# A decay-scaled triangle and a normalization in a Mamba-2 scan, written by ScalarE in place of VectorE

## The chip, the core and the metric

The kernel runs on one core of one Trainium2 chip. The metric is the device time of one execution in microseconds (us). PE is TensorE, DVE is VectorE, ACT is ScalarE, POOL is GpSimd and SP is SyncE. A profile is of one execution, taken by the hardware profiler.

## The reference, cut to what matters

The program is a two-layer decoder trunk over 512 tokens and 1024 features in float32: sparse attention, SwiGLU, a Mamba-2 (SSD) mixer, SwiGLU. The change is in the mixer's chunked scan, of which this is the core (chunks of 128 tokens, 4 groups of 8 heads, head size 64, state size 128):

```
def step(state, inp):
    cum = jnp.cumsum(dtc * A, axis=1)
    seg = cum[:, :, None] - cum[:, None]
    L = jnp.exp(jnp.where(tril, seg, -jnp.inf))
    cb = jnp.einsum('btgn,bsgn->btsg', cc, bc)
    y_diag = jnp.einsum('btsgh,bsghp->btghp', cb[..., None] * L, xdt)
    y_off = jnp.einsum('btgn,bghpn->btghp', cc, state) * jnp.exp(cum)[..., None]
    ...
    return new_state, y_diag + y_off
...
y = y + d_skip[..., None] * xs
yg = y * silu(z)                                   # per group of 512 features
yg = yg * rsqrt(mean(yg * yg) + EPS)               # over the group
return (yg * norm_w) @ w_out
```

## The kernel before, in words

Each engine has its own program, written out by hand in order; they meet only in semaphores. An engine runs its instructions in program order, so a wait holds everything behind it.

The scan runs over 16 tiles: 4 groups `g` of heads, and in each 4 chunks of tokens `k` (called tiles 0 to 3 of a group below). The group function of each engine is called for group 0, in a loop for groups 1 and 2, and for group 3 with `last=True` (`scan_groups`, L294). In every tile the engines do this:

- The decays of tile `k+1`. `build_g` (L1532) writes `Gm`: for each of 8 heads the 128x128 triangle `tri[:, 0]` times one number per partition (`dt * A` of that head), four heads (128x512) to an instruction and two instructions (`q`) to a tile. It is called two tiles ahead. PE multiplies `Gm` with a second triangle (L744) into two PSUM banks, ACT takes the exponential into `Lx` (`decays`, L1083), POOL multiplies it with the masked product of C and B (L1725).
- The inputs of tile `k+1`: POOL makes `xdt`, `dxs` and `xdd` (L1717 to L1720), ACT packs B and C (`stage`, L1076), PE multiplies and transposes them (L748, L749), DVE copies them out (`stage`, L1540).
- The output of tile `k`: PE multiplies with the state (L793), forms the state's increment (L796), and does eight small products with `Lx` (L802). DVE scales, adds and gates: L1591, L1593 and L1594 (the state), L1600, L1602, and L1605, which multiplies by `zs` and signals `y_done`.
- The normalization of tile `k`: ACT sums the squares (L1124), DVE makes the mean (L1550), POOL the power -1/2 (`rstd`, L1636, signal `y_rs`), and DVE multiplies the 128x512 tile `ybuf` by it (`scale_y`, L1552, an instruction at L1555, signal `y_scaled`). PE transposes the result (L756), DVE copies it to `yT` (L1561).

PE has other work in the scan: the projection `z` of the next group (L772), 24 products of 128x512 to a tile, in thirds of 8, placed around the scan's own products. They fill one PSUM bank; ACT copies it out (`z_copy`, L1096) before the next tile's may start (signal `evac`). In tile 0 of a group all three thirds stand at the end. The `z` products of tile 0 need new weights from their 13th on, those of tile 3 release a weight buffer. A weight chunk is split by ACT (`split_hi`, L827) and then DVE (`split_lo`, L1152), in tile 0 and in tile 3. In tile 0 of groups 1 to 3 ACT also turns `zraw` into `zs` by Silu over 2048 columns (L1116), with a load of the activation table before it. Group 3 has no `z`; there ACT and DVE split parts of `yT` instead (L1121, L1611), and after tile 3 the output projection starts (L354 to L356 with `yh`, `yl`).

ACT's order in a tile is `z_copy` of the tile before, the weight split (tile 0), the exponentials, `stage`, Silu (tile 0) or the weight split (tile 3) or L1121 (last group), then the sum of squares. DVE's is mean, `stage`, `scale_y` of the tile before, `build_g`, the weight split (tiles 0 and 3), L1591 to L1605, L1561, L1611 (last group).

Of the kernel before, what the change touches and what calls it, by code (L numbers as in the profile page):

```python
# [27 lines left out]
ALU = mybir.AluOpType  # L28
ACT = mybir.ActivationFunctionType
AX = mybir.AxisListType.X  # L30

P = 128
SEQ, DM = 512, 1024
TT = SEQ // P
# [7 lines left out]
SH, SG, SHP, SP_, SN = 32, 4, 8, 64, 128  # L42
# [67 lines left out]
def trunk(nc, wstream, xT_in, cols_in, rows_in, pos_in, cw1_in, cw2_in, ident_in, tri_in, cmask_in, out):  # L110
    with ExitStack() as ctx:
# [177 lines left out]
        def after(engine, semaphore, value):  # L289

            if not isinstance(value, int) or value > 0:
                engine.wait_ge(semaphore, value)

        def scan_groups(engine, group, enter=None, leave=None):  # L294

            group(0, False)
            with engine.Fori(0, SG - 2) as i:
                if enter:
                    enter(i)
                group(i + 1, False)  # L300
            if leave:
                leave()
            group(SG - 1, True)
# [515 lines left out]
        def _(act):  # L819
            A = act.activation  # L820

            def split_hi(n, i=None, per=0):

                act.wait_ge(landed[n % 2], 16 * (n // 2 + 1) if i is None else i * (8 * per) + 16 * (n // 2 + 1))
                if n >= 2:
                    act.wait_ge(products, at(2 * (n - 1), i, 2 * per))
                A(wh[:, n % 2, :], wraw[:, n % 2, :], ACT.Copy).then_inc(hi_done, 1)  # L827
# [248 lines left out]
            def stage(g, j):  # L1076

                c = j % TT
                after(act, y_mm, g * 8 + 2 * (j - 3))
                A(bc[:, c, :, :], BCf[:, :, bass.ds(g + j // TT, 1), c * P:(c + 1) * P].rearrange("p b a n -> p (b a) n"),  # L1080
                  ACT.Copy).then_inc(staged, 1)

            def decays(g, j):  # L1083
                for q in range(2):
                    act.wait_ge(seg_mm, g * 8 + (2 * j + q + 1))
                    after(act, y_mm, g * 8 + 2 * (j - 1))
                    A(Lx[:, j % 2, q, :, :], ps[:, q, :].rearrange("p (h t) -> p h t", h=4), ACT.Exp
                      ).then_inc(seg_exp, 1)

            def z_copy(g, tt):  # L1090

                if tt in (-1, 3):
                    act.wait_ge(products, g * 4 + (2 * n0 + 4 + tt + 1))
                else:
                    act.wait_ge(z_mm, g * 3 + (tt + 1))
                A(zraw[:, tt % TT, :], ps[:, 5, :], ACT.Copy, scale=stat[:, 4 + tt % TT:5 + tt % TT]).then_inc(evac, 1)  # L1096

            def group(g, last):
                first = isinstance(g, int) and g == 0
                for k in range(TT):  # L1100
                    if k:
                        if not last:
                            z_copy(g, k - 1)
                    elif not first:
                        z_copy(g, -1)
                    if k == 0:
                        split_hi(n0 + 3, g, 2)
                    if k < 3 or not last:
                        decays(g, k + 1)
                    if k < 2 or not last:  # L1110
                        stage(g, k + 2)
                    if k == 0:
                        if not first:
                            act.wait_ge(evac, g * 4 + (t0 + 4))
                            act.wait_ge(y_done, g * 4)
                            A(zs[:, :, :], zraw[:, :, :], ACT.Silu).then_inc(z_silu, 1)  # L1116
                    if k == 3 and not last:
                        split_hi(n0 + 4, g, 2)
                    if last:
                        act.wait_ge(yT_done, 9 + k)  # L1120
                        A(yh[:, k, 0:12, :], yT[:, k, 0:12, :], ACT.Copy).then_inc(yh_done, 1)  # L1121
                    act.wait_ge(y_done, g * 4 + (k + 1))
                    after(act, y_sq, g * 4 + k)
                    A(ysq[:, :], ybuf[:, k % 2, :], ACT.Square, accum_out=yst[:, k % 2, 0:1]).then_inc(y_sq, 1)  # L1124
            stage(0, 0)
            stage(0, 1)
            decays(0, 0)
            split_hi(n0 + 2)
            for tt in range(TT):
                act.wait_ge(products, 2 * n0 + 3 + tt // 2)  # L1130
                A(zs[:, tt, :], ps[:, 2 + tt, :], ACT.Silu, scale=stat[:, 4 + tt:5 + tt]).then_inc(evac, 1)
            scan_groups(act, group)
            act.wait_ge(yT_done, 4 * SG)
            A(yh[:, :, 12:16, :], yT[:, :, 12:16, :], ACT.Copy).then_inc(yh_done, 1)
            residual("ssm_out")
# [4 lines left out]
        def _(dve):  # L1140
# [388 lines left out]
            n0 = CHUNK["z"]  # L1529


            def build_g(g, j):  # L1532

                for q in range(2):
                    after(dve, seg_mm, g * 8 + (2 * j + q - 1))
                    at_ = g * SHP + ((j // TT) * SHP + (j % TT) * SH + 4 * q)
                    TTo(Gm[:, q, :, :], tri[:, 0, :].unsqueeze(1).broadcast_to([P, 4, P]),
                        dtb[:, 1, bass.ds(at_, 4)].unsqueeze(2).broadcast_to([P, 4, P]), ALU.mult).then_inc(g_built, 1)

            def stage(g, j):  # L1540

                dve.wait_ge(cb_mm, g * 4 + (j + 1))
# [5 lines left out]
            def y_mean_square(g, j):  # L1548
                dve.wait_ge(y_sq, g * 4 + (j + 1))
                TS(yst[:, j % 2, 1:2], yst[:, j % 2, 0:1], 1.0 / GW, EPS, ALU.mult, ALU.add).then_inc(y_var, 1)  # L1550

            def scale_y(g, j):  # L1552
                dve.wait_ge(y_rs, g * 4 + (j + 1))
                y = ybuf[:, j % 2, :]
                TS(y, y, yst[:, j % 2, 2:3], None, ALU.mult).then_inc(y_scaled, 1)  # L1555

            def to_features(g, j):
                dve.wait_ge(yT_mm, g * 4 + (j + 1))
# [8 lines left out]
            def group(g, last):  # L1567
                first = isinstance(g, int) and g == 0

                def per_head(n, c):  # L1570
                    return ex[:, n, bass.ds(g * SHP + c * SH, SHP)].unsqueeze(2).broadcast_to([P, SHP, SP_])
                for k in range(TT):
                    if k or not first:
                        y_mean_square(g, k - 1)
                    if k < 3 or not last:
                        stage(g, k + 1)
                    if k or not first:
                        scale_y(g, k - 1)
                    if k < 2 or not last:
                        build_g(g, k + 2)  # L1580
                    if k == 0:
                        split_lo(n0 + 3, g, 2)
                    if k == 3 and not last:
                        split_lo(n0 + 4, g, 2)
                    y = ybuf[:, k % 2, :]
                    after(dve, yT_mm, g * 4 + (k - 1))
                    if k < 3:
                        dve.wait_ge(state_mm, g * 3 + (k + 1))
                    if k:
                        dve.wait_ge(y_mm, g * 8 + (2 * k + 1))  # L1590
                        V.inc(TTo(heads(y), heads(ps[:, 3, :]), per_head(0, k), ALU.mult))  # L1591
                    if k in (1, 2):
                        step(TTo(heads(state[:, :]), heads(state[:, :]), per_head(2, k), ALU.mult))  # L1593
                        TTo(state[:, :], state[:, :], ps[:, 4, :], ALU.add).then_inc(state_done, 1)  # L1594
                    if k == 0:
                        dve.tensor_copy(state[:, :], ps[:, 4, :]).then_inc(state_done, 1)
                    dve.wait_ge(y_mm, g * 8 + 2 * (k + 1))
                    dve.wait_ge(xdt_done, g * 12 + 3 * (k + 1))
                    V.wait(dve)
                    step(TTo(y, y if k else dxs[:, k % 2, :], ps[:, 2, :], ALU.add))  # L1600
                    if k:
                        step(TTo(y, y, dxs[:, k % 2, :], ALU.add))  # L1602
                    if k == 0 and not first:
                        dve.wait_ge(z_silu, g)
                    TTo(y, y, zs[:, k, :], ALU.mult).then_inc(y_done, 1)  # L1605
                    if k or not first:
                        to_features(g, k - 1)
                    if last:
                        dve.wait_ge(yh_done, k + 1)
                        dve.wait_ge(yT_done, 9 + k)  # L1610
                        TTo(yl[:, k, 0:12, :], yT[:, k, 0:12, :], yh[:, k, 0:12, :].bitcast(F32), ALU.subtract  # L1611
                            ).then_inc(yl_done, 1)
            build_g(0, 0)
            dve.wait_ge(cum_exp, 1)
            stage(0, 0)
            build_g(0, 1)
            split_lo(n0 + 2)
            scan_groups(dve, group, lambda i: V.enter(i, DVE_SCAN_STEPS), lambda: V.leave(SG - 2, DVE_SCAN_STEPS))
            y_mean_square(SG - 1, 3)
            scale_y(SG - 1, 3)  # L1620
            to_features(SG - 1, 3)
            dve.wait_ge(yh_done, TT + 1)
            TTo(yl[:, :, 12:16, :], yT[:, :, 12:16, :], yh[:, :, 12:16, :].bitcast(F32), ALU.subtract).then_inc(yl_done, 1)
# [210 lines left out]
```

## Time and profile before

| | |
|---|---|
| median of 3 runs | 1614.51 us (1613.33 to 1615.09) |
| the profiled execution | 1612.59 us, span 1610.8 us |
| PE busy | 1508.9 us (94%) |
| DVE busy | 853.7 us (53%) |
| ACT busy | 630.9 us (39%) |
| POOL busy | 261.2 us (16%) |
| mean granted PE clock | 0.982 |

The span runs from the first to the last instruction; busy shares are of the span. Times of single rows are microseconds from the span's start. The scan stands between about 943 and 1148 us.

### The profile page before, as it was taken

To read this page: it belongs to the slowest core of one execution; us is meant where nothing else is said; L and a number is where in the kernel's file an instruction comes from. 1 tells how busy PE (TensorE), PEld (TensorE's weight loads), DVE (VectorE), ACT (ScalarE), POOL (GpSimd) and SP (SyncE) were. 2 spreads that over 40 slices of the span, in tenths; PEclk is the share of its full clock that TensorE was granted. 3 is DMA by queue.
4 is the path that set the end of the run, shared out by engine and by line. 5 is a ranking of instruction groups with operands and counts; after the bars stand their busy time and mean duration, and the time that the engine had idled before them with its cause. 6 is when DMAs were issued, how large, how long until landed. Compare 5 with 4: busy or idle time off the path is not lost.

```text
span 1610.8 us, 20549 instructions
## 1 busy us (share of the span) xinstructions
PE 1508.9 (94%) x7469; PEld 1217.9 (76%) x7469; DVE 853.7 (53%) x1137; ACT 630.9 (39%) x895; POOL 261.2 (16%) x289
## 2 busy tenths in 40 slices
PE   6989889778999999999999999998799999999999
PEld 5777667656788888788788867665687888887887
DVE  4556767663444444333397758789623444444222
ACT  4445655653343433323233352444223344343111
POOL 4133242301100000001000026666211000000000
PEclk9989999999999999999999999999799999999999
DMA  7200101102222222222222220111022222222222
GB/s 310 79 27 1 53 12 40 52 1 79 79 105 98 84 104 104 80 103 104 105 105 79 102 81 27 53 52 53 4 101 79 105 79 104 91 91 104 105 105 78
DMA packets 19198, 129.47 MB, mean 80 GB/s; under 512 B 2256, under 2 KB 2896, under 8 KB 4560
## 3 DMA queue, kind: packets, MB, share of 16 engines
q1 hardware_dynamic: 19008, 126.75, 21.9%
q10 hardware_dynamic: 144, 2.10, 0.4%
q8 instruction: 30, 0.49, 0.1%
q14 instruction: 16, 0.13, 0.0%
HBM read 126.74 MB, written 2.10 MB: 80 GB/s over the span
## 4 chain that ended last, share of the span: by engine, by line
PE 82%; issue 6%; DVE 5%; POOL 5%; ACT 2%; DVEq 0%; POOLq 0%; ACTq 0%
PE ps L354 22%; PE ps L356 22%; PE ps L355 22%; PE ps L624 3%; PE ps L607 2%; PE ps L772 2%; PE ps L587 2%; POOL Lx L1725 2%; POOL sqacc L1650 1%; PE ps L550 1%; PE ps L744 1%; PE ps L603 1%; PE ps L802 1%; DVE sm L1370 1%; PE ps L551 1%
## 5 line engine op out<-in xcount | busy, mean ns | idle before, releaser
L1152 DVE TENSOR_TENSOR wl<-wraw,wh 128x2048 fp32r<-128x2048 f32 x112 | 264.5, 2362 | 274.0 <-ACT wh L827 273.9
L354 PE MATMUL ps<-xh,wh 128*128 128x512 f32 (+2 forms) x912 | 359.3, 394 | 6.1 <-DVE xl L1162 3.4
L355 PE MATMUL ps<-xl,wh 128*128 128x512 f32 (+2 forms) x912 | 356.2, 391 | 0.0
L356 PE MATMUL ps<-xh,wl 128*128 128x512 f32 (+2 forms) x912 | 356.2, 391 | 0.0
L827 ACT ACTIVATE wh<-wraw 128x2048 fp32r<-128x2048 f32 x112 | 213.9, 1910 | 185.3 <-PE ps L356 175.5
L354 PEld LDWEIGHTS ps<-xh,wh 128*128 128x128 f32 (+2 forms) x912 | 170.8, 187 | 44.3 <-issue 4.5
L356 PEld LDWEIGHTS ps<-xh,wl 128*128 128x128 f32 (+2 forms) x912 | 170.7, 187 | 37.4
L355 PEld LDWEIGHTS ps<-xl,wh 128*128 128x128 f32 (+2 forms) x912 | 170.8, 187 | 37.0 <-issue 0.7
L354 PE MATMUL ps<-hh,wh 128*128 128x512 f32 x352 | 137.9, 392 | 4.1 <-DVE hid L1232 4.1
L355 PE MATMUL ps<-hl,wh 128*128 128x512 f32 x352 | 137.6, 391 | 0.0
L356 PE MATMUL ps<-hh,wl 128*128 128x512 f32 x352 | 137.5, 391 | 0.0
L1650 POOL TENSOR_TENSOR sqacc<-sqacc,sq 128x512 f32<-128x512 f32 x32 | 44.2, 1381 | 481.9 <-ACT sq L836 480.9
L889 ACT ACTIVATE hh<-hid 128x512 f32 x44 | 27.8, 632 | 189.7 <-DVE hid L1232 189.7
L1370 DVE TENSOR_REDUCE sm<-ps 128x2 f32<-128x256 f32 (+3 forms) x64 | 52.6, 822 | 67.6 <-PE ps L545 40.9
L354 PEld LDWEIGHTS ps<-hh,wh 128*128 128x128 f32 x352 | 66.4, 189 | 18.8 <-DVE hid L1232 5.0
L982 ACT ACTIVATE PT<-ps 128x256 f32<-128x256 f32 (+3 forms) x64 | 45.0, 704 | 83.0 <-PE ps L587 82.7
L355 PEld LDWEIGHTS ps<-hl,wh 128*128 128x128 f32 x352 | 66.5, 189 | 13.9
L356 PEld LDWEIGHTS ps<-hh,wl 128*128 128x128 f32 x352 | 66.5, 189 | 13.8
L974 ACT ACTIVATE Pm<-ps,sm 128x128 f32<-128x128 f32 (+3 forms) x128 | 66.1, 526 | 9.3 <-DVE sm L1370 9.2
L885 ACT ACTIVATE gate<-gate 128x512 f32<-128x512 f32 x44 | 27.7, 632 | 102.0 <-DVE gate L1225 102.0
L1195 DVE TENSOR_TENSOR xT<-ps,xT 128x512 f32<-128x512 f32 (+1 forms) x32 | 22.1, 690 | 85.7 <-PE ps L356 77.2
L587 PE MATMUL ps<-ident,Pm 128*128 128x128 f32 x320 | 47.3, 279 | 17.7 <-DVE Pm L1381 15.9
(262 smaller groups left out, 2491.1 us busy)
## 6 DMA issues: line engine op xcount, KB each, us to landing
wraw<-wstream SPq DMA_DIRECT2D x112, 1024.0 KB, 4.8
cw<-cw_in SPq DMA_DIRECT2D x1, 4096.0 KB, 18.9
xT<-xT_in SPq DMA_DIRECT2D x4, 512.0 KB, 8.1
xT<-xT_in ACTq DMA_DIRECT2D x1, 2048.0 KB, 8.5
out<-xT SPq DMA_DIRECT2D x8, 256.0 KB, 6.5
rows<-rows_in SPq DMA_DIRECT2D x1, 276.0 KB, 10.5
tri<-tri_in SPq DMA_DIRECT2D x1, 192.0 KB, 10.5
cmask<-cmask_in SPq DMA_DIRECT2D x1, 128.0 KB, 10.0
```

What stands on the lines that cost most here:

```text
L354: mm(o, wa[0], xa[0], start=start, stop=False)
L355: mm(o, wa[0], xa[1], start=False, stop=False)
L356: return mm(o, wa[1], xa[0], start=False, stop=stop)
L587: ins = pe.transpose(ps[:, 4 + b, j * P:(j + 1) * P], Pm[:, s % 2, b, j * P:(j + 1) * P], ident[:, :])
L607: ins = mm(o, vst[:, j, b, :], PT[:, h % 2, b, j, q], start=False, stop=b == 1 and j == i)
L624: ins = mm(ps[:, 7, :], (xh, xl, xh)[pss][:, kt, t], (wh, wh, wl)[pss][:, slot, w], start=m == 0, stop=m == 23)
L827: A(wh[:, n % 2, :], wraw[:, n % 2, :], ACT.Copy).then_inc(hi_done, 1)
L974: A(Pm[:, s % 2, b, 0:w], src, ACT.Exp, bias=sm[:, 4, m + b:m + 1 + b], accum_out=sm[:, 4, m + 4 + b:m + 5 + b]).then_inc(expd, 1)
L982: A(PT[:, h % 2, :, 0:i + 1, i * P:(i + 1) * P], ps[:, 4:6, 0:(i + 1) * P].rearrange("p b (j q) -> p b j q", q=P), ACT.Copy).then_inc(pT_d ...
L1152: TTo(wl[:, s, :], wraw[:, s, :], wh[:, s, :].bitcast(F32), ALU.subtract).then_inc(lo_done, 1)
L1370: dve.tensor_reduce(sm[:, 4, m:m + 2], src.rearrange("p (b n) -> p b n", b=2) if i < 2 else src, AX, ALU.max, negate=True).then_inc(negmax, 1)
L1650: TTo(sqacc[:, :], sqacc[:, :], sq[:, mt % 2, :], ALU.add).then_inc(acc_done, 1)
```

## The change

`build_g` and `scale_y` move from DVE's program to ACT's. `build_g` becomes eight ACT instructions of 128x128 to a tile in place of two DVE instructions of 128x512: an activation Copy takes one scale for each partition, so each head is an instruction of its own. `scale_y` stays one instruction of 128x512. Their places in ACT's order are new: `scale_y` of the tile before stands first in a tile, ahead of `z_copy`; `build_g` stands between the exponentials and `stage`. At the start `build_g(0, 0)` stands behind the exponential of the cumulative sums (L1074) and ahead of `stage(0, 0)`, where DVE did it before them.

```
@@ block.scalar
+            def build_g(g, j):
+                for q in range(2):
+                    after(act, seg_mm, g * 8 + (2 * j + q - 1))
+                    at_ = g * SHP + ((j // TT) * SHP + (j % TT) * SH + 4 * q)
+                    for h in range(4):
+                        a = dtb[:, 1, at_ + h:at_ + h + 1] if isinstance(at_, int) else dtb[:, 1, bass.ds(at_ + h, 1)]
+                        ins = A(Gm[:, q, h, :], tri[:, 0, :], ACT.Copy, scale=a)
+                    ins.then_inc(g_built, 1)
+            def scale_y(g, j):
+                act.wait_ge(y_rs, g * 4 + (j + 1))
+                y = ybuf[:, j % 2, :]
+                A(y, y, ACT.Copy, scale=yst[:, j % 2, 2:3]).then_inc(y_scaled, 1)
...
                 for k in range(TT):
+                    if k or not first:
+                        scale_y(g, k - 1)
                     if k:
                         if not last:
                             z_copy(g, k - 1)
...
                     if k < 3 or not last:
                         decays(g, k + 1)
+                    if k < 2 or not last:
+                        build_g(g, k + 2)
                     if k < 2 or not last:
                         stage(g, k + 2)
...
+            act.wait_ge(dt_done, 1)
+            build_g(0, 0)
             stage(0, 0)
             stage(0, 1)
             decays(0, 0)
+            build_g(0, 1)
             split_hi(n0 + 2)
...
             scan_groups(act, group)
+            scale_y(SG - 1, 3)
@@ block.vector
-            def build_g(g, j):
-                for q in range(2):
-                    after(dve, seg_mm, g * 8 + (2 * j + q - 1))
-                    at_ = g * SHP + ((j // TT) * SHP + (j % TT) * SH + 4 * q)
-                    TTo(Gm[:, q, :, :], tri[:, 0, :].unsqueeze(1).broadcast_to([P, 4, P]),
-                        dtb[:, 1, bass.ds(at_, 4)].unsqueeze(2).broadcast_to([P, 4, P]), ALU.mult).then_inc(g_built, 1)
-            def scale_y(g, j):
-                dve.wait_ge(y_rs, g * 4 + (j + 1))
-                y = ybuf[:, j % 2, :]
-                TS(y, y, yst[:, j % 2, 2:3], None, ALU.mult).then_inc(y_scaled, 1)
...
-                    if k or not first:
-                        scale_y(g, k - 1)
-                    if k < 2 or not last:
-                        build_g(g, k + 2)
...
-            build_g(0, 0)
             dve.wait_ge(cum_exp, 1)
             stage(0, 0)
-            build_g(0, 1)
             split_lo(n0 + 2)
...
             y_mean_square(SG - 1, 3)
-            scale_y(SG - 1, 3)
             to_features(SG - 1, 3)
```

## Rows read from the trace of the kernel before

**Rows 1.** Windows: start:end, us, then each engine's busy us (instructions), PE clock, DMA
```profile
1063.60:1112.00 48.40, 44.56 (x212) 32.28 (x211) 40.80 (x51) 19.89 (x31) 30.78 (x25) 1.00 0.12 44
1112.00:1148.30 36.30, 21.11 (x82) 13.69 (x80) 33.34 (x41) 13.44 (x19) 19.11 (x15) 0.76 0.09 29
```
**Rows 2.** Instruction groups by line and form, DVE: busy us, mean ns, idle before
```profile
L1537 DVE TENSOR_TENSOR Gm<-tri,dtb 128x512 f32<-128x512 f32 x32 | 45.5, 1461 | 0.0
L1555 DVE TENSOR_SCALAR ybuf<-ybuf,yst 128x512 f32<-128x512 f32 x16 | 14.7, 917 | 2.4 <-POOL yst L1636 2.1
```
**Rows 3.** Instruction groups by line and form, ACT: the nearest form for `scale_y`
```profile
L841 ACT ACTIVATE xh<-xT,cols 128x512 fp32r<-128x512 f32 x24 | 15.8, 708 | 0.0
```
**Rows 4.** Timeline of ACT (start us, us): two 128x128 with an operand per partition
```profile
91.82 0.62 ACT L955 ACTIVATE hidK<-ps,cols 128x128 f32<-128x128 f32 x2
```
**Rows 5.** Timeline of PE, tiles 0 to 3 of group 2
```profile
1067.23 0.50 PE L772 MATMUL ps<-wh,xh 128*128 128x512 f32 x1 [2.71 <-DVE wl L1152]
...
1072.07 0.47 PE L772 MATMUL ps<-wh,xh 128*128 128x512 f32 x1
...
1087.24 1.90 PE L802 MATMUL ps<-xdt,Lx 128*128 128x64 f32 x16
...
1095.12 0.47 PE L772 MATMUL ps<-wh,xh 128*128 128x512 f32 x1
```
**Rows 6.** Timeline of DVE: end of group 1, tiles 0 and 2 of group 2
```profile
1057.43 0.69 DVE L1605 TENSOR_TENSOR ybuf<-ybuf,zs 128x512 f32<-128x512 f32 x1
...
1068.41 0.69 DVE L1605 TENSOR_TENSOR ybuf<-ybuf,zs 128x512 f32<-128x512 f32 x1
...
1088.45 0.69 DVE L1591 TENSOR_TENSOR ybuf<-ps,ex 128x512 f32<-128x512 f32 x1 [0.18 <-PE ps L802]
...
1092.03 0.69 DVE L1605 TENSOR_TENSOR ybuf<-ybuf,zs 128x512 f32<-128x512 f32 x1
```
**Rows 7.** The chain that ended last: POOL's power, and `z` of tile 1, group 1
```profile
1024.86 1.84 PE ps L772 x8
...
1059.15 0.56 POOL yst L1636
```
**Rows 8.** Timeline of ACT around the start of group 2
```profile
1058.16 0.63 ACT L1124 ACTIVATE ysq<-ybuf 128x512 f32<-128x512 f32 x1 [5.51 <-DVE ybuf L1605]
...
1058.79 0.67 ACT L1096 ACTIVATE zraw<-ps,stat 128x512 f32<-128x512 f32 x1
1059.36 1.90 ACT L827 ACTIVATE wh<-wraw 128x2048 fp32r<-128x2048 f32 x1
...
1063.85 1.91 ACT L1116 ACTIVATE zs<-zraw 128x2048 f32<-128x2048 f32 x1
```
**Rows 9.** Timeline of PE where the scan starts
```profile
948.44 1.98 PE L744 MATMUL ps<-Gm,tri 128*128 128x512 f32 x4 [0.58 <-ACT ex L1074]
...
950.51 0.47 PE L354 MATMUL ps<-wh,xh 128*128 128x512 f32 x1
```
**Rows 10.** Timeline of DVE: ends of groups 0 and 2, tiles 0 and 2 of group 3
```profile
1008.40 0.69 DVE L1605 TENSOR_TENSOR ybuf<-ybuf,zs 128x512 f32<-128x512 f32 x1
...
1105.09 0.69 DVE L1605 TENSOR_TENSOR ybuf<-ybuf,zs 128x512 f32<-128x512 f32 x1
...
1116.06 0.69 DVE L1605 TENSOR_TENSOR ybuf<-ybuf,zs 128x512 f32<-128x512 f32 x1
...
1132.74 0.69 DVE L1591 TENSOR_TENSOR ybuf<-ps,ex 128x512 f32<-128x512 f32 x1
...
1136.74 1.63 DVE L1605 TENSOR_TENSOR ybuf<-ybuf,zs 128x512 f32<-128x512 f32 x1
```
**Rows 11.** Timeline of PE: tile 2 of group 3 and the output projection's first product
```profile
1128.40 2.07 PE L793 MATMUL ps<-state,bc 128*128 128x512 f32 x2 [2.99 <-DVE ybuf L1605]
...
1148.31 0.80 PE L354 MATMUL ps<-yh,wh 128*128 128x512 f32 x1 [3.65 <-DVE yl L1611]
```
**Rows 12.** Windows (columns as in Rows 1): the products behind PE's wait in group 1
```profile
1018.20:1022.80 4.60, 4.60 (x13) 3.66 (x14) 2.58 (x5) 0.72 (x2) 2.79 (x4) 0.63 0.65 228
```

## The prediction

> **What bounds the kernel now.** I read the table of windows first. In group 2 of the scan PE is busy 44.56 of 48.40 us and DVE 40.80, ACT only 19.89; in group 3, which has no `z` products, DVE is busy 33.34 of 36.30 and PE 21.11 [rows 1]. So the scan has two stages with different limits: groups 0 to 2 go by PE, group 3 by DVE's list together with the waits between it and PE. Then the groups of instructions: what the change takes off DVE is 45.5 us of `build_g` and 14.7 of `scale_y` [rows 2], 60 us in all. That isn't the gain. The timelines say which wait ends last. In tile 2 of group 2 DVE's L1591 was itself released by PE [rows 6], so with two instructions fewer ahead of it, it starts no sooner. The one wait of PE inside groups 1 and 2 is 2.71 us for the weight split in tile 0 [rows 5].
>
> ACT is idle more than half the time, but the question is what now stands in its queue ahead of what PE needs: `z_copy` (PE's next `z` products wait for it), the weight split, and in tile 0 the Silu that L1605 waits for.
>
> **Prices of the moved work.** `scale_y`: 0.71 us, as L841, the same form [rows 3], and the next instruction starts 0.1 sooner than it ends, so 0.61 in a queue. A `build_g` instruction is 128x128 with a scale per partition. From L841's 0.708 less 384 columns at (1.91 - 0.63) / 1536 = 0.83 ns [rows 8] one alone is 0.39. Two short ones of that kind in a row took 0.62 together [rows 4], so the second adds 0.23 to 0.31. I take 0.29 from start to start, 2.3 us for the eight of a tile; ends 0.25 and 0.39 (2.0 and 3.1 us). In the loop each has its scale's address from a register, which no row shows for such short ones; that is why the upper end goes without any overlap.
>
> **1. The start.** `Gm` was ready long before; now ACT makes it after L1074. PE's L744 began at 948.44 and the products behind it at 950.51 [rows 9]. Now 2.3 us of `build_g` lie ahead, of which PE's first half of L744 (1.0 us) hides one, and `stage` behind it puts 0.2 more ahead of L748. The second half of L744 can start at about 950.8, the products at 952.0: **+1.5** (ends 1.2 and 2.3). Everything behind moves with it, since PE is full there.
>
> **2. Tiles 1 to 2 and 2 to 3 of groups 0 to 2.** A new wait stands first in ACT's tile: `scale_y` waits for `y_rs`, and `z_copy` is behind it. From `y_done` (1057.43 + 0.69 = 1058.12 [rows 6]) `z_copy` started 0.67 later [rows 8]; the power ended 1.59 later (1059.15 + 0.56 [rows 7]). Now `scale_y` starts at 1.63, `z_copy` at 2.24, ends at 2.91, and PE's next `z` products start at 2.97 after `y_done`. In tile 2 of group 2 L802 started at 1087.24, `y_done` came at 1092.72 [rows 5, 6], 5.48 later; 5.48 + 2.97 = 8.45, where PE by its own list starts `z` after 7.88 (1095.12 [rows 5]). PE so waits 0.57. As DVE's chain may run a little faster with less beside POOL, the ends are 0 and 0.6; I take 0.4, six times: **+2.4**. Behind `z_copy` stand the exponentials, `build_g`, `stage`; `Gm` and `Lx` are wanted a tile later, so they are covered.
>
> **3. Tile 3.** ACT's weight split waits for the 12th `z` product, so there was idle time of ACT before it; `build_g` (2.3) makes it about 0.4 late. DVE's half then runs after POOL's products rather than beside them, which gives 0.4 to 0.6 back: **0** (ends -0.2 and +0.6, thrice).
>
> **4. Tile 0 of groups 1 and 2.** Here ACT's queue is longest: `scale_y`, `z_copy`, split, exponentials, `build_g`, `stage`, table load, Silu. Silu ended 1063.85 + 1.91 - 1058.12 = 7.64 after `y_done` [rows 6, 8]. New: 0.96 waiting for `y_rs` (1.63 - 0.67), 0.61 for `scale_y`, 2.32 for `build_g`: 11.53. L1605 of tile 0, which started at 1068.41, 10.29 after [rows 6], now starts at 11.58 and ends at 12.27; the tail of step 2 (2.97) puts PE's `z` of tile 1 at 15.24. Before it was 1072.07 - 1058.12 = 13.95 in group 2 [rows 5, 6], so +1.3; in group 1 it was 1024.86 - 1009.09 = 15.77 [rows 7, 10], because PE's clock was granted at 0.63 behind its 2.71 us wait [rows 12]; that slow stretch would now be hidden: -0.5. Together **+0.8**. The old 2.71 us wait for the weights shrinks (DVE's split no longer stands behind `build_g`), but what it gives is taken by the wait for `z_copy` and buys nothing. PE is then idle twice, some 2 us each.
>
> **5. Group 3.** From `y_done` of group 2 (1105.78) to the output projection (1148.31) it was 42.53 us [rows 10, 11]. Tile 0 ends later for the Silu, at 12.27 against 10.97 (1116.75). From there DVE has less in its list (`scale_y` and `build_g` no longer stand ahead of L1591) and the loop is PE to DVE to PE: from L793 to L1591 4.34 us (1128.40 to 1132.74), then DVE's chain, 4.27 us where POOL was quiet (1088.45 to 1092.72 [rows 6]) and 5.63 where it read beside it (1132.74 to 1138.37 [rows 10]). I take 4.8 twice: `y_done` at 21.4 and 30.6, and from there as before 9.94 (1138.37 to 1148.31): 40.5. **-2.0** (ends -3.1 with 4.27 twice, -0.4 with 5.63). ACT's L1121 now stands behind `build_g` and ahead of the sum of squares and can hold that up, but only `stage` on DVE and POOL's inputs hang on it, and I count these as done before L1591 is released.
>
> L1605 took 1.63 us beside POOL's products in tile 2 of this group and 0.69 elsewhere [rows 10, 6]. The Trainium skill ("SBUF — State Buffer", section "SBUF: two separate sides") says that VectorE, in an instruction with two SBUF inputs, and GpSimd reading SBUF hold a shared port in turn, and that "the other fully blocks". By that rule L1602 and L1605 meet POOL's `Lx` in both tiles whatever else DVE has dropped, and the sum would be 1.6 higher than mine, 1619.6.
>
> **6. The clock.** Two more waits of about 2 us in each of groups 1 and 2 can bring the lower level as the 2.71 us one did once in two. At 0.63 twelve products took 4.6 us [rows 12] where they need 2.8 at the full level, some 1.6 to 1.8. Behind the weights it is hidden, behind `z_copy` it isn't. I add half of one: **+0.8**.
>
> **7. The end.** The last `scale_y` and its transpose lie behind the first products of the projection: 0.
>
> The sum is 1.5 + 2.4 + 0 + 0.8 - 2.0 + 0.8 = +3.5. The profiled execution took 1612.59 us (span 1610.8), which makes 1616.1; the median stands 1.9 above it, so **1618.0**.
>
> **Rivals.** *DVE was the bound (faster).* If the Silu, or whatever ACT does in tile 0, ended by 10 us after `y_done`, group 3 would lose what leaves DVE's list: four `scale_y` of 0.92 and four `build_g` instructions of 1.46 [rows 2], 9.5 us, less 1.5 of the start: 8.0, 1606.5. For it: DVE's 92% in group 3. Against it: the queue of step 4, whose length comes from rows. *The queue hides better than I think (no change).* Step 2 gives 0, group 3 gives 3.1: 1.5 + 0.8 - 3.1 = -0.8, 1613.7. For it: step 2 is a difference of 0.57 between two sums of 8. *The eight instructions don't overlap (slower still).* 0.39 each adds 0.8 to a tile: at the start, in tile 0 of groups 1 to 3, in tile 3 of groups 0 to 2 (0.6 of it) and in tile 1 of group 3: 0.8 + 2.4 + 1.8 + 0.8 = 5.8, 1623.8. For it: register addresses; against it: rows 4.
>
> **How the numbers follow.** A measurement of this kernel tells about 0.2%, 3.2 us, from no change. My forecast has a chance of 0.58, own range 1614.5 to 1622; the faster rival 0.13; no change 0.15; the slower one 0.14. Faster by over 0.2% (under 1611.3) is the first rival and a little of the second, 0.15; within 0.2% (to 1617.7) is the rest of the second and the lower part of my own range, 0.34; slower is 0.51. Range 1610 to 1625.
>
> **What would show it.** Right: eight ACT instructions at 0.29 spacing; PE waits for L1096 before its first `z` product in tiles 1 to 3, about 2 us in tile 1 and under 0.6 in the others; L1605 of tile 0 waits for the Silu, near 12.3 after `y_done`; group 3 two us shorter. Wrong: no such waits of PE, L1605 of tile 0 released by something on DVE or PE, or group 3 shorter by over 5 us.

## The result, and the profile after

The changed kernel takes 1620.93 us (median of 7 runs, 1617.74 to 1622.19), the kernel before 1615.09 beside it (7 runs, 1613.33 to 1615.64). The ratio is 1.0036 with a 95% interval of 1.0026 to 1.0045: slower by 5.8 us, and by 4.2 to 7.3 with the interval. Forecast were 1618.0 and +3.5.

The profiled execution of the changed kernel, at 1622.19 us, is the slowest of its seven, that of before (1612.59) the fastest of its own. So the two traces differ by 9.6 us, more than the medians do. Of all executions behind the medians in this text two were disturbed and are left out of the ratios, though not of the medians: one of the kernel with Silu first (2560.44 us) and one of the kernel before (1750.42). Busy time moved as meant: DVE from 853.7 to 791.6 us, ACT from 630.9 to 677.1. The two moved groups, by line and form (busy us, mean ns, idle before):

```profile
L1097 ACT ACTIVATE Gm<-tri,dtb 128x128 f32<-128x128 f32 x128 | 39.1, 397 | 0.0
L1103 ACT ACTIVATE ybuf<-ybuf,yst 128x512 f32<-128x512 f32 x16 | 11.6, 722 | 18.5 <-POOL yst L1639 18.5
```

Against [rows 2] ACT needs 51 us of busy time for what cost DVE 60, and it waits another 18.5 us for the power of POOL, sixteen times, ahead of whatever stands behind `scale_y`. (L1605 of before is L1611 in this kernel, L1725 is L1728.)

To see where the time is, I cut the scan at the same events in every trace: the first product with `dtb` on PE (L736), the first `z` product behind it, `y_done` of tile 3 of groups 0, 1 and 2 (start plus duration of the instruction that multiplies by `zs`), the first product of the output projection, and the end. All in us:

| kernel | start | to the end of group 0 | group 1 | group 2 | group 3 | rest |
|---|---|---|---|---|---|---|
| before | 3.48 | 58.58 | 49.03 | 47.66 | 42.53 | 462.49 |
| changed | 4.95 | 58.93 | 52.22 | 51.09 | 42.13 | 463.80 |
| only `build_g` moved | 4.96 | 58.05 | 45.33 | 45.33 | 40.88 | 464.00 |
| only `scale_y` moved | 3.48 | 58.63 | 47.34 | 47.40 | 41.02 | 462.41 |
| changed, `z_copy` first | 4.95 | 58.06 | 46.38 | 46.39 | 40.57 | 463.46 |
| changed, Silu first | 4.95 | 58.89 | 48.47 | 48.48 | 41.53 | 463.91 |
| changed, 10 idle products | 4.95 | 58.95 | 50.34 | 50.34 | 42.38 | 463.19 |
| changed, 7 idle products | 4.95 | 58.91 | 49.41 | 49.43 | 41.51 | 462.81 |
| changed, last `build_g` early | 4.94 | 58.91 | 49.41 | 50.98 | 41.14 | 463.62 |
| only `build_g` moved, start on DVE | 3.48 | 58.06 | 45.33 | 45.34 | 41.46 | 463.05 |
| changed, `z_copy` first, start on DVE | 3.48 | 58.09 | 46.40 | 46.39 | 41.56 | 463.65 |
| moved in group 3 alone | 3.48 | 58.61 | 49.03 | 47.69 | 38.06 | 463.18 |
| best | 3.48 | 58.05 | 45.32 | 45.32 | 39.58 | 463.98 |

Not in the table is what lies ahead of the scan. The same code there ended between 944.10 us (last `build_g` early) and 951.65 (only `build_g` moved) in these thirteen traces, and the rest, also the same code, took 462.41 to 464.00. So a stage of one trace may be set against the same stage of another, but the total of one execution says little. Group 3 with the same instructions took 42.13, 42.38 and 41.51 us (changed, 10 and 7 idle products), so less than a microsecond there is no difference either.

The waits of PE in the scan of the changed kernel (who waited for whom, us in total, times, longest):

```profile
PE ps L744 <- ACT Gm L1097: 8.1, 3, 3.4
PE ps L793 <- DVE ybuf L1611: 6.2, 2, 4.6
PE ps L772 <- ACT zraw L1111: 6.2, 2, 3.1
PE ps L354 <- DVE yl L1617: 3.6, 1, 3.6
PE ps L772 <- DVE wl L1175: 1.6, 2, 0.8
```

The 2.71 us wait for the weights [rows 5] is down to 0.8, and 3.1 us for `z_copy` stands in its place, in tile 1 of groups 1 and 2. ACT's timeline at the start of group 2 shows why (start us, us):

```profile
1063.42 0.63 ACT L1143 ACTIVATE ysq<-ybuf 128x512 f32<-128x512 f32 x1 [5.13 <-DVE ybuf L1611]
...
1064.99 0.72 ACT L1103 ACTIVATE ybuf<-ybuf,yst 128x512 f32<-128x512 f32 x1 [0.85 <-POOL yst L1639]
1065.61 0.67 ACT L1111 ACTIVATE zraw<-ps,stat 128x512 f32<-128x512 f32 x1
1066.18 1.90 ACT L827 ACTIVATE wh<-wraw 128x2048 fp32r<-128x2048 f32 x1
1067.99 1.07 ACT L1087 ACTIVATE Lx<-ps 128x512 f32<-128x512 f32 x2
1068.94 2.45 ACT L1097 ACTIVATE Gm<-tri,dtb 128x128 f32<-128x128 f32 x8
...
1073.01 1.91 ACT L1135 ACTIVATE zs<-zraw 128x2048 f32<-128x2048 f32 x1
1075.75 0.63 ACT L1143 ACTIVATE ysq<-ybuf 128x512 f32<-128x512 f32 x1 [0.83 <-DVE ybuf L1611]
...
1077.32 0.72 ACT L1103 ACTIVATE ybuf<-ybuf,yst 128x512 f32<-128x512 f32 x1 [0.85 <-POOL yst L1639]
1077.94 0.67 ACT L1111 ACTIVATE zraw<-ps,stat 128x512 f32<-128x512 f32 x1
```

From `y_done` (1063.38) to here ACT has no idle time but 0.85 us for the power, twice, and 0.83 for L1611 (the lines left out are short ones and a load of the activation table, 1.28 us). Compare [rows 8]: there `z_copy` came 0.67 after `y_done`, here 2.23, and the Silu ends 11.54 after it, not 7.64. On DVE and PE the same stretch reads:

```profile
1075.02 0.69 DVE L1611 TENSOR_TENSOR ybuf<-ybuf,zs 128x512 f32<-128x512 f32 x1 [3.42 <-ACT zs L1135]
```

```profile
1070.46 0.50 PE L772 MATMUL ps<-wh,xh 128*128 128x512 f32 x1 [0.79 <-DVE wl L1175]
...
1078.66 0.50 PE L772 MATMUL ps<-wh,xh 128*128 128x512 f32 x1 [3.11 <-ACT zraw L1111]
```

`y_done` of tile 0 now hangs on the Silu, and `z` of tile 1 starts 15.28 after `y_done` of the group before (13.95 before).

What comes behind those two waits is PE at the lower of its two clock levels (0.50 where it holds for a whole window, 1.2 of 2.4 GHz). Windows of the changed kernel (columns as in [rows 1]), behind the wait in group 1 and in group 2:

```profile
1026.44:1029.00 2.56, 2.56 (x6) 2.08 (x7) 0.00 (x0) 2.55 (x5) 2.25 (x3) 0.50 0.00 0
1029.00:1032.91 3.91, 3.91 (x7) 1.94 (x7) 0.00 (x0) 2.42 (x9) 1.88 (x2) 0.57 0.00 0
...
1078.60:1081.00 2.40, 2.33 (x9) 1.88 (x9) 0.00 (x0) 2.37 (x5) 2.10 (x3) 0.83 0.00 0
1081.00:1084.00 3.00, 3.00 (x6) 1.20 (x4) 0.00 (x0) 2.64 (x10) 2.09 (x2) 0.57 0.00 0
```

### The profile page after: what moved, and what is told of

The parts are those of the page before. It is cut to its first block, busy times and chain, and to the rows that moved or that the text cites. A ratio compares the mean times of both kernels' runs of the same rounds, so it can differ in the third digit from the quotient of the medians.

```text
span 1620.4 us, 20685 instructions
## 1 busy us (share of the span) xinstructions
PE 1513.7 (93%) x7469; PEld 1218.5 (75%) x7469; DVE 791.6 (49%) x1089; ACT 677.1 (42%) x1039; POOL 243.3 (15%) x289
## 4 chain that ended last, share of the span: by engine, by line
PE 82%; issue 7%; POOL 4%; DVE 4%; ACT 3%; DVEq 0%; POOLq 0%; ACTq 0%
PE ps L354 22%; PE ps L356 22%; PE ps L355 22%; PE ps L624 3%; PE ps L607 2%; PE ps L772 2%; PE ps L587 2%; POOL Lx L1728 1%; PE ps L744 1%; PE ps L802 1%; PE ps L550 1%; POOL sqacc L1653 1%; PE ps L603 1%; PE ps L551 1%; DVE sm L1393 1%
## 5 line engine op out<-in xcount | busy, mean ns | idle before, releaser
L1175 DVE TENSOR_TENSOR wl<-wraw,wh 128x2048 fp32r<-128x2048 f32 x112 | 258.4, 2307 | 304.6 <-ACT wh L827 304.4
## 6 DMA issues: line engine op xcount, KB each, us to landing
cmask<-cmask_in SPq DMA_DIRECT2D x1, 128.0 KB, 10.4
```

The source lines that it names most:

```text
L1175: TTo(wl[:, s, :], wraw[:, s, :], wh[:, s, :].bitcast(F32), ALU.subtract).then_inc(lo_done, 1)
```

## The experiments

My theory after the result: nothing that was moved is dear. ACT's order makes one queue of the wait for `y_rs`, `scale_y`, `z_copy`, `build_g` and the Silu, and PE waits at its end, at times with a lowered clock behind it. The rivals stand in the expectations.

**One part alone.** The first kernel has `scale_y` back on DVE, the second `build_g`:

```diff
# only build_g moved: ACT
-                    if k or not first:
-                        scale_y(g, k - 1)
... the last scale_y (tile 3 of group 3) goes from here too
# and DVE, behind stage(g, k + 1), as before
+                    if k or not first:
+                        scale_y(g, k - 1)
... and the last one
```

> The changed kernel with scale_y back on DVE: only build_g is on ACT. Theory (what costs is one queue on ACT in tile 0: the wait for y_rs, scale_y and build_g all stand ahead of the Silu, and z_copy stands behind scale_y): build_g alone puts the Silu's end at 7.6 + 2.3 = 10.0 us after y_done, just what L1605 had before, so nothing is left of the 3 us waits of PE for z_copy and only the start (+1.5) and a gain in group 3 remain: 1613.5 to 1616.5, no difference from before. Rival (the eight short instructions cost by themselves, wherever they stand; parts add up): the larger part of the 5.8 us remains, 1618 to 1620.

```diff
# only scale_y moved: ACT
-                    if k < 2 or not last:
-                        build_g(g, k + 2)
# and DVE, as before (build_g(0, 0) and build_g(0, 1) too)
+                    if k < 2 or not last:
+                        build_g(g, k + 2)
```

> The changed kernel with build_g back on DVE (the start too): only scale_y is on ACT. Theory: the six waits of PE for z_copy in tiles 2 and 3 (0.2 to 0.6 us each) stay, +1 to +2.4, no long wait in tile 1, since the Silu ends near 9.2 after y_done; group 3 gets back three scale_y of DVE, -3: 1613 to 1616. Rival (parts add up): what build_g alone leaves of the 5.8 us, 1617 to 1619.

Measured: 1607.29 us (ratio to before 0.995, interval 0.9937 to 0.9963) and 1608.02 (0.9959, 0.9945 to 0.9972). Both expectations of mine are missed, on the good side, and the rival falls altogether: each part alone gains 7 us, and both together lose 6. Most of why they gain is in the waits of PE in groups 1 and 2: before, one of 2.71 us for the weights in each [rows 5]. In group 1 with `build_g` alone, and with `scale_y` alone, all that is left is:

```profile
PE ps L772 <- ACT zraw L1106: 0.9, 1, 0.9
```

```profile
PE ps L772 <- DVE wl L1160: 1.2, 1, 1.2
PE ps L772 <- ACT zraw L1101: 0.8, 1, 0.8
```

Without `build_g` (2.98 us) or `scale_y` (1.26) ahead of the weight split DVE has the weights sooner; I had expected tile 1 to start when it did before, though that start was itself late by the 2.71 us. With `build_g` alone both groups take 45.33 us: 2.3 less than before in group 2 and 3.7 in group 1, where before had the clock's fall as well. Group 3, which has none of these waits, gives another 1.6 and 1.5 us in the table.

**ACT's order.** One kernel has the changed kernel's `z_copy` ahead of `scale_y`, so that it doesn't wait for POOL's power; another has `build_g` behind the Silu.

```diff
+                    if k:
+                        if not last:
+                            z_copy(g, k - 1)
+                    elif not first:
+                        z_copy(g, -1)
                     if k or not first:
                         scale_y(g, k - 1)
-                    if k:
-                        if not last:
-                            z_copy(g, k - 1)
-                    elif not first:
-                        z_copy(g, -1)
```

> The changed kernel with z_copy ahead of scale_y in ACT's order, nothing else. Theory: PE's waits for z_copy go in tiles 1 to 3 (3.1 us in tile 1 twice, 0.2 to 0.5 six times), and with them the fall of the clock behind the two long ones (1.3 to 1.7 each, in some executions): 1620.9 - 6 - 1 - 2 = 1612 to 1615. Rival (the Silu behind build_g sets the pace by holding y_done, not z_copy): PE then waits for y_done at L793 instead; gain under 2 us, 1619 to 1621.

```diff
-                    if k < 2 or not last:
-                        build_g(g, k + 2)
                     if k < 2 or not last:
                         stage(g, k + 2)
                     if k == 0:
                         ... Silu
+                    if k < 2 or not last:
+                        build_g(g, k + 2)
```

> The changed kernel with build_g behind the Silu in tile 0 (and in the other tiles behind stage), z_copy still behind scale_y. Theory: y_done of tile 0 comes 2.3 us sooner, PE's two long waits shrink from 3.1 to 0.8 and the clock holds: 1620.9 - 4.6 - 1.5 = 1614 to 1616.5. Rival (z_copy behind scale_y is the whole cost, or Gm is then late for PE's L744): 1619 to 1621.

`z_copy` first: 1608.61 (0.9967, 0.9953 to 0.998). Swapping two instructions of ACT gives 12.3 us back, more than I expected, and makes a kernel slower than before into a faster one. By the table 3.0 us a group of it is waiting (46.4 us against the 49.4 that a group of the changed kernel takes at the full clock, see below), and some 4.5 is the clock. Its waits in group 1 are these, and its clock doesn't fall behind them:

```profile
PE ps L772 <- ACT zraw L1111: 1.3, 1, 1.3
PE ps L772 <- DVE wl L1175: 0.4, 1, 0.4
```

Silu first: 1616.96 (1.0013, 1.0003 to 1.0024), 4.0 less than the changed kernel and a little above the range that I expected. Group 1 takes 48.47 us, and what is left stands in the waits of PE over the whole scan: the Silu is out of the way, but now `Gm` comes late.

```profile
PE ps L744 <- ACT Gm L1097: 9.8, 5, 6.9
...
PE ps L772 <- ACT zraw L1111: 2.6, 2, 1.3
```

So of the two, the order of `z_copy` is the larger part: the wait for POOL's power belongs behind whatever PE waits for.

**The clock.** Into PE's wait for `z_copy` I put products whose result nobody reads. The wait isn't shortened by them.

```diff
# tile 1 of groups 1 and 2; ten, in the second kernel seven
+                    if k == 1 and not last and not (isinstance(g, int) and g == 0):
+                        for _ in range(10):
+                            mm(ps[:, 3, 0:256], ident[:, :], tri[:, 0:2, :].rearrange("p a b -> p (a b)"), start=True, stop=True)
                     z_at(0)
```

> The changed kernel with ten more products of 128x256 on PE, thrown away, in tile 1 of groups 1 and 2, where PE waits 3.1 us for z_copy. They take some 2.1 us and put no result anywhere that is read. Theory: PE's clock isn't lowered behind that wait any more, and the lowered stretch (0.50 to 0.60, 1.3 to 2.3 us of PE's time in each group) goes: groups 1 and 2 from 52.2 and 51.1 us to about 49.5, 1620.9 - 3 to 4 = 1617 to 1618. Rival (the clock isn't part of it; the length of the wait alone is): the same 1620.9, or more by what the products delay.

> As with ten thrown-away products in tile 1 of groups 1 and 2 of the changed kernel, but seven. Ten took 4.1 us of PE where 3.1 were idle, and groups 1 and 2 came to 50.3 us each; seven take 2.9. Theory: the clock is held all the same, groups 1 and 2 come to 49.4 us, 1617.0 to 1618.2. Rival (fewer let the clock fall in some executions): as the changed kernel, 1619 to 1621.

Ten: 1619.15 (1.0037, 1.0023 to 1.0052), groups 1 and 2 at 50.34 us. The trace has the full clock, but the ratio is that of the changed kernel, so by its time this kernel misses what I expected. The products ran longer than I had reckoned, 4.14 us to the next start where I took 2.1, and longer than the wait of 3.1:

```profile
1022.44 4.48 PE L790 MATMUL ps<-tri,ident 128*128 128x256 f32 x20
1026.58 0.58 PE L772 MATMUL ps<-wh,xh 128*128 128x512 f32 x1
```

Seven: 1616.18 (1.0010, 0.9999 to 1.0020), a little below what I expected, groups 1 and 2 at 49.41 and 49.43. The same 49.41 stands in group 1 of the kernel with the last `build_g` early, which has no such product: there the clock held by itself in that execution (windows; before, at and behind the wait):

```profile
1018.00:1023.00 5.00, 2.11 (x8) 0.92 (x6) 1.94 (x5) 3.32 (x5) 1.70 (x3) 1.00 0.25 103
1023.00:1026.00 3.00, 2.77 (x10) 1.99 (x11) 0.00 (x0) 2.97 (x6) 2.69 (x3) 1.00 0.00 0
```

So 49.4 us is a group's length with the full clock, and its fall cost 2.8 and 1.7 us in the two groups of the changed kernel's trace. With seven idle products the kernel is 4.7 us faster by the medians (1620.93 against 1616.18; the kernel before had 1615.09 and 1614.41 beside them). That the whole difference is the clock's isn't shown; single runs of the kernel with seven products went up to 1622.88. Nor is it shown beyond doubt that the products hold the clock: it was full behind all four waits with them, and behind one of four without them (two in the changed kernel's trace, two in that of the last `build_g` early).

**Group 3.** The `build_g` for its tile 3 goes first in tile 1, where ACT waits for the power anyway, and from its old place:

```diff
                 for k in range(TT):
+                    if last and k == 1:
+                        build_g(g, 3)
                     if k or not first:
                         scale_y(g, k - 1)
```

> The changed kernel with one build_g moved: in the last group, the one for tile 3 stands first in tile 1, ahead of scale_y and the exponentials. Theory (group 3 gained nothing because PE's L744 for tile 3, which waits 2.9 us for Gm, stands ahead of L793 of tile 2): that wait goes and group 3 falls from 42.1 to about 40 us, 1618 to 1619.5. Rival (group 3 is held by DVE beside POOL, whatever Gm does): no change, 1620.5 to 1621.5.

1619.34 (1.0029, 1.0018 to 1.0040), whose interval overlaps that of the changed kernel; in the traces group 3 falls from 42.13 to 41.14 us, half of what I expected and little more than the same code differs by. PE in the changed kernel, and then in this one:

```profile
1126.84 1.12 PE L793 MATMUL ps<-state,bc 128*128 128x512 f32 x2 [1.61 <-DVE ybuf L1611]
...
1134.21 3.26 PE L744 MATMUL ps<-Gm,tri 128*128 128x512 f32 x4 [2.90 <-ACT Gm L1097]
...
1137.90 1.17 PE L793 MATMUL ps<-state,bc 128*128 128x512 f32 x2
```

```profile
1120.71 2.07 PE L793 MATMUL ps<-state,bc 128*128 128x512 f32 x2 [1.07 <-DVE ybuf L1613]
...
1126.85 1.96 PE L744 MATMUL ps<-Gm,tri 128*128 128x512 f32 x4 [0.34 <-ACT Lx L1087]
1130.97 1.12 PE L793 MATMUL ps<-state,bc 128*128 128x512 f32 x2 [1.84 <-DVE ybuf L1613]
```

L793 of tile 2 no longer stands behind the wait for `Gm`, but now waits for `y_done` itself. Part of the missing half is the clock: from 1120.7 to 1124.0 it was granted at 0.50. L793 of tile 1 took 2.07 us in this execution and 1.12 in the other, and DVE's L1599, which PE releases, started 4.60 us behind it (1125.31) in place of 2.96.

**The start, and where the gain can be had.** Three more kernels. The first two are the `build_g` kernel and the `z_copy` one with the first two `build_g` back on DVE (the diff is that of the change, reversed, at the start):

> build_g on ACT, scale_y on DVE (1607.3 as such), and the first two build_g before the groups back on DVE. Theory: the start's 1.5 us is plainly on the path, since ACT makes Gm while PE waits: 1605.3 to 1606.3. Rival (something behind it hides the start, such as the wait for the Silu of z at the end of that stage): 1607 to 1607.5.

> Both moved, z_copy ahead of scale_y (1608.6 as such), and the first two build_g back on DVE. Theory: -1.5, 1606.6 to 1607.6. Rival as for the other: 1608.3 to 1608.9.

1605.87 (0.9948, 0.9935 to 0.9961) and 1608.66 (0.9961, 0.9948 to 0.9973). The start is 3.48 us again in both traces. The first median is 1.4 us lower, as expected, the second no lower; with intervals of some 4 us neither tells 1.5 us from nothing, so the gain is shown by the start's column of the table alone. In the second kernel's trace group 3 took 41.56 us against 40.57, with the same instructions in it. What differs is where the clock was low. PE with `z_copy` first, and then with the start on DVE too:

```profile
1114.68 2.07 PE L793 MATMUL ps<-state,bc 128*128 128x512 f32 x2 [2.01 <-DVE ybuf L1611]
...
1122.05 2.29 PE L744 MATMUL ps<-Gm,tri 128*128 128x512 f32 x4 [1.77 <-ACT Gm L1097]
```

```profile
1113.80 1.13 PE L793 MATMUL ps<-state,bc 128*128 128x512 f32 x2 [1.69 <-DVE ybuf L1616]
...
1121.16 3.40 PE L744 MATMUL ps<-Gm,tri 128*128 128x512 f32 x4 [2.90 <-ACT Gm L1097]
```

`Gm` is there at the same time after `y_done` of group 2 in both. In the first the lower level falls into tile 1 and L744 of tile 2 runs at the full one; in the second it falls on L744 (granted clock 0.60 from 1121 to 1124), and L793 behind it starts 23.00 us after that `y_done`, not 22.06.

> The kernel before, with the move made in the last group alone: scale_y on ACT there, and the build_g of its tile 3 on ACT, first in tile 1; everything else on DVE as before. Theory (of the gain of the single moves, groups 1 and 2 make most by PE's shorter wait for the weights, and group 3 some 1.5 to 2.5 us): 1612 to 1613.5. Rival (the gain lies in group 3, where DVE was 92% busy): 1608 to 1610.

```diff
# ACT, the kernel before
+                    if last and k == 1:
+                        build_g(g, 3)
                     if k:
                         ... z_copy
+                    if last:
+                        scale_y(g, k - 1)
# DVE
-                    if k or not first:
+                    if (k or not first) and not last:
                         scale_y(g, k - 1)
-                    if k < 2 or not last:
+                    if k < 1 or not last:
                         build_g(g, k + 2)
```

1609.10 (0.9959, 0.9946 to 0.9973). Here the rival was right: group 3 alone, taken off DVE's list, falls to 38.06 us, 4.5 less than before, more than I had thought was there. Groups 1 and 2 stay at 49.03 and 47.69, as in the kernel before.

> build_g on ACT in groups 0 to 2 and in tile 0 of group 3, the first two on DVE; scale_y on DVE except in tiles 1 to 3 of the last group; the last build_g first in tile 1 of the last group. Theory (each engine's queue is short where the other waits for it): groups 1 and 2 stay at 45.3 us, group 3 falls from 41.5 to about 39.5, 1605.9 - 1.5 = 1603.5 to 1605. Rival (group 3 is held by DVE's chain beside POOL, so that two instructions less change nothing): 1605.5 to 1606.5.

It is the kernel with `build_g` on ACT and the start on DVE, and in the last group:

```diff
+                    if last and k == 1:
+                        build_g(g, 3)
+                    if last and k:
+                        scale_y(g, k - 1)
```

1603.99 us, ratio 0.9934 (0.9921 to 0.9948): 10.4 us less than before beside it (1614.41), faster than both kernels and within what I expected. Groups 1 and 2 take 45.32 us and group 3 39.58.

## Why the prediction was right, and which terms were off

The direction, the place and the mechanism came out as forecast, and the median lies in the range; the size was too small, 3.5 against 5.8. That it came so near is in part luck, for errors of both signs stand in it: group 3 gave less back than I had reckoned, group 0 cost less, and the clock, which differs from execution to execution, cost more. The numbers below are from the changed kernel's slowest execution, so they add up to more than 5.8. By its steps:

- **Prices.** `scale_y` took 0.72 us (0.71 said), eight `build_g` 2.44: (2.44 - 0.40) / 7 = 0.29 us from start to start, as taken. The addresses from registers cost nothing, and the rival of eight that don't overlap falls by these rows.
- **Step 1**, +1.5: 4.95 - 3.48 = 1.47.
- **Steps 2 and 3**, +0.8 in group 0: 0.35. The waits were sized well: tile 2's `y_done` came 11.83 us after tile 1's (985.82 and 997.65), where before it came 11.45 after (984.47 and 995.92), which is 0.4; it is too short to show among the waits. With `z_copy` first group 0 takes 58.06, 0.9 less than with the change. What I had left out is that this is also 0.5 less than before, as it is with `build_g` moved alone (58.05).
- **Step 4**: `y_done` of tile 0 at 12.33 (12.27 said), `z` of tile 1 at 15.28 (15.24), L1611 waiting for the Silu, PE for `z_copy`. With the clock held the groups are 49.4 each, where steps 2 to 4 gave 49.03 + 0.3 = 49.3 and 47.66 + 2.1 = 49.8.
- **Step 5**, -2.0: -0.4. This is a step that failed. DVE's chain took 5.73 and 5.77 us beside POOL (1129.80 to 1135.53, 1140.90 to 1146.67), not 4.8, which makes 1.9. And I left out that L744, which waits for `Gm`, stands in PE's list ahead of L793: that start came 2.4 after `y_done`. In the other direction PE ran at the full clock there in this execution and came from L793 to L1597 in 3.0 us, not 4.3. Two more traces with the same group 3 (the ones with idle products) give -0.2 and -1.0 for this step. From the rule of the Trainium skill that I set beside it ("SBUF — State Buffer", section "SBUF: two separate sides"), by which a DVE instruction with two SBUF inputs and a GpSimd one that reads SBUF can't run together and the one that starts later waits, I had worked out that DVE would be held up in both tiles. On this the trace agrees with it, though not on which instructions: L1611 took 1.64 us in the first of the tiles, and in the second 0.69, where L1599 and L1608 took 1.54 each.

```profile
1141.51 1.54 DVE L1599 TENSOR_TENSOR state<-state,ex 128x512 f32<-128x512 f32 x1
...
1144.40 1.54 DVE L1608 TENSOR_TENSOR ybuf<-ybuf,dxs 128x512 f32<-128x512 f32 x1
```

- **Step 6**, +0.8: this term was the one most mis-sized. I had PE idle for 2.0 us ahead of `z_copy` and the clock falling once in four. It was idle for 3.1 us, since the weights came 1 us sooner than I had reckoned (DVE's split took 2.29 us, no longer 3.37), and in the profiled execution the clock fell both times, which cost 4.5 us. It also stayed low longer behind the scan (granted clock 0.78 from 1160.3 to 1164.3, where before had 1.00 as far behind its scan), and the rest is 1.3 us longer, which is within what the rest differs by in any of the kernels. Seven runs of the changed kernel spread over 4.5 us, those of before over 2.3; how much of that is the fall in the scan isn't shown, since the code ahead of the scan alone differs by more. Without the clock my sum was +2.7; the kernel with seven idle products is at +1.8 beside before.

The rival of a DVE that bounds group 3 was closer to something true than I gave it credit for: in the last group alone it is worth 4.5 us. The changed kernel can't collect it: its `y_done` of tile 0 comes 2.0 us later than in that kernel (12.33 and 10.37 after `y_done` of group 2), for ACT's tile 0, and its tile 2 takes 2.0 longer (11.14 and 9.10), where PE waits for `Gm`.

## What to carry to other kernels

An instruction moved to an idle engine costs what stands behind it in that engine's order, and above all the wait that it brings along. Here a wait of 0.85 us for a third engine stood ahead of a copy that frees PSUM, and swapping the two was worth 12 us, some 4.5 of them the clock's. Price two moves to the same queue together: each alone took 7 us off, both together put 6 on. And when a wait of PE goes, ask what the start behind it would be without it, not when it was.

## What the runs showed of the hardware

In groups 1 and 2 PE's granted clock stayed at 1.00 behind waits of 1.3 us (`z_copy` first), fell once in two behind one of 2.71 (before, and moved in group 3 alone: in group 1 and not in group 2, both times), and both times behind 3.1 us in one execution (changed), once in two in another (last `build_g` early). With 4.1 or 2.9 us of thrown-away products in that wait it was 1.00 behind it in the one profiled execution of each such kernel. VectorE's weight split in tile 0 of groups 1 to 3 took 2.29 us in the changed kernel and 3.37 before. In group 3 it started at 1119.20, ahead of POOL's first product with `Lx` at 1119.80, and before at 1111.47, behind that product's start at 1110.96; so it may be who comes first that decides, which no run tested.
